# A hybrid decoder layer: the last unit's last eight gathered rows are fetched in two parts

## The reference

```python
# per token and head (8 heads): 16 expert ids and their softmax gates
ue = jnp.take(u_tab, idb, axis=0)
h = jnp.einsum('thkd,td->thk', ue, xb)
act = gb * jax.nn.gelu(h, approximate=False)
ve = jnp.take(v_tab, idb, axis=0)
ffn = jnp.einsum('thk,thkd->td', act, ve)
...
x = layer_norm(DEEPNORM_ALPHA * x + ffn, ln2_g, ln2_b)
gate = jax.nn.sigmoid(x @ ple_wgate + ple_bgate)
x = layer_norm(DEEPNORM_ALPHA * x + gate * (p @ ple_wproj), ln3_g, ln3_b)
```

## Time and profile before

| | |
|---|---|
| three runs, median (lowest to highest) | 1473.62 us (1471.78 to 1478.03) |
| the profiled execution, its own time | 1475.97 us |
| its span, first to last instruction | 1473.9 us |
| busy: PE / DVE / ACT / POOL | 77% / 72% / 64% / 40% of the span |
| DMA queue of the gathers | 536.90 MB, 87.1% of 16 engines' span |
| mean granted TensorE clock | 0.884 |

### The profile page before, as it was taken

One profiled execution on the slowest core, in us unless ns is written; L12 is line 12 of the kernel. 1 busy time (PEld: TensorE's weight loads), 2 busy tenths in 40 slices (PEclk: granted clock), 3 DMA queues, 4 the chain that ended last, 5 costly groups with the idle time before them and its releaser, 6 DMA issues.

```text
span 1473.9 us, 18837 instructions
## 1 busy us (share of the span) xinstructions
PE 1141.0 (77%) x6795; PEld 894.0 (61%) x6795; DVE 1065.0 (72%) x2592; ACT 949.8 (64%) x1613; POOL 584.5 (40%) x528
## 2 busy tenths in 40 slices
PE   8998999988768877787667876786677766677666
PEld 3556777767666667665645555665555655655545
DVE  1378776668778786778756776877886886687765
ACT  2236677678887888766636677667556666666652
POOL 1043344334443444434423444454344444443440
PEclk9999999999899988999767988999888887799888
DMA  9589999999999999999999999999999999999990
GB/s 370 229 320 398 425 417 378 427 427 426 426 427 425 426 424 421 426 427 427 421 429 426 414 423 426 417 418 427 426 421 426 426 425 422 426 418 413 396 426 33
DMA packets 88390, 593.45 MB, mean 403 GB/s; under 512 B 9533, under 2 KB 14309, under 8 KB 19050
## 3 DMA queue, kind: packets, MB, share of 16 engines
q0 software_dynamic: 73728, 536.90, 87.1%
q1 hardware_dynamic: 14570, 55.36, 9.3%
HBM read 590.13 MB, written 2.10 MB: 402 GB/s over the span
## 4 chain that ended last, share of the span: by engine, by line
DMA 42%; PE 29%; ACT 11%; DVE 10%; POOL 4%; issue 4%; SPq 0%; POOLq 0%; DVEq 0%; ACTq 0%
DMA arena<-in_uv,ids 41%; PE ps L1007 10%; DVE arena L1524 6%; PE ps L727 5%; ACT arena L1214 5%; POOL arena L547 4%; PE ps L562 3%; PE ps L909 2%; ACT actv L1209 2%; PE ps L836 2%; PE ps L573 2%; ACT L1206 1%; ACT L1259 1%; ACT gel L1206 1%; PE ps L640 1%
## 5 line engine op out<-in xcount | busy, mean ns | idle before, releaser
L547 POOL DMA_INDIRECT arena<-in_uv,ids x512 | 579.4, 1132 | 811.4 <-PE ps L1007 681.6
L1007 PE MATMUL ps<-ident,arena 128*128 128x128 f32 x4096 | 617.1, 310 | 307.4 <-ACT arena L1214 301.9
L1524 DVE CUSTOM_DVE_ANT_0 arena<-arena 128x1024 f32<-128x1024 f32 x512 | 622.8, 1224 | 287.3 <-DMA arena<-in_uv,ids 279.4
L1007 PEld LDWEIGHTS ps<-ident,arena 128*128 128x128 f32 x4096 | 539.1, 160 | 405.1 <-ACT arena L1214 337.0
L1214 ACT ACTIVATE arena<-arena,actv 128x1024 f32<-128x1024 f32 x511 | 555.8, 1135 | 0.0
L1206 ACT ACTIVATE gel<-hid 128x2 f32<-128x2 f32 (+1 forms) x256 | 51.9, 203 | 387.3 <-DVE hid L1524 381.1
L1209 ACT ACTIVATE actv<-gel,gates 128x1 f32<-128x1 f32 x511 | 122.8, 287 | 8.4
L727 PE MATMUL ps<-arena 128*128 128x128 f32 x992 | 127.3, 291 | 0.0
L727 PEld LDWEIGHTS ps<-arena 128*128 128x128 f32 x992 | 125.3, 209 | 0.0
L1206 ACT ACT_TABLE_LOAD x51 | 65.4, 1283 | 6.8 <-DVE gates L1466 5.9
L836 PE MATMUL ps<-arena 128*128 128x384 f32 x192 | 67.1, 493 | 0.0
(11 more groups left out here) (207 smaller groups left out, 930.5 us busy)
## 6 DMA issues: line engine op xcount, KB each, us to landing
arena<-in_wq SPq DMA_DIRECT2D x20, 1024.0 KB
arena<-in_uv,ids POOLq DMA_INDIRECT x512
arena<-in_w_out SPq DMA_DIRECT2D x2, 2048.0 KB, 16.2
arena<-in_w_gate SPq DMA_DIRECT2D x1, 4096.0 KB
arena<-in_w_out SPq DMA_DIRECT2D x3, 1024.0 KB, 13.4
arena<-in_w_k SPq DMA_DIRECT2D x4, 512.0 KB, 7.0
arena<-in_w_q SPq DMA_DIRECT2D x2, 1024.0 KB, 10.6
arena<-in_w_gv SPq DMA_DIRECT2D x1, 2048.0 KB, 11.9
```

The costliest lines, as they stand in the source:

```text
L547: nc.gpsimd.indirect_dma_start(out=rows[:, c % RING, :], out_offset=None, in_=a["uv"][:, :], in_offset=bass.IndirectOffsetOnAxis(ap=ids[:, ...
L1007: i = mm(ps[:, run_bank(r) + k // 4, (k % 4) * P:(k % 4 + 1) * P], rows[:, c % RING, D + k * P:D + (k + 1) * P], ident[:, :], is_transpose ...
L1524: v.tensor_tensor_reduce(out=r, in0=r, in1=x1[t], scale=1.0, scalar=0.0, op0=ALU.mult, op1=ALU.add, accum_out=hid[:, i, c:c + 1]).then_inc ...
```

## The change

In the last unit the fetches c = 8 to 15 are cut. The main part brings columns 0 to 1535 (all of u and the first half of v, `PART` = 1536, 6 KB a row). Eight further indirect DMAs, issued behind all others, bring the late parts: columns 1536 to 2047, 2 KB a row. ScalarE scales and PE sums only the first half of v for these eight. The second halves are scaled and added up by VectorE in token order (`add_late`: one `tensor_scalar`, then seven `scalar_tensor_tensor` of 128x512, all into `late_sum`); PE then transposes the sum (4 blocks) into bank 5, and VectorE adds it to `acc`. The second half of what PE had summed up to fetch 7 is added to `acc` earlier, beside the last unit (`add_half(1, ...)` at g == 6). The order of PE's tail changes too: the first half of `acc` is transposed back and the first two gate quarters opened before the late sum is there; the second half is transposed back between quarters 2 and 3.

```diff
+LATE = TOPK - RING
+PART = D + HALF
+        late_sum = rows[:, LATE % RING, PART:2 * D]
...
+                    n = PART if u == NU - 1 and c >= LATE else 2 * D
                     nc.gpsimd.indirect_dma_start(
-                        out=rows[:, c % RING, :], out_offset=None, in_=a["uv"][:, :],
+                        out=rows[:, c % RING, 0:n], out_offset=None, in_=a["uv"][:, :],
...
             for u in range(NU):
                 gather_unit(u)
+            for c in range(LATE, TOPK):
+                nc.gpsimd.indirect_dma_start(
+                    out=rows[:, c % RING, PART:2 * D], out_offset=None, in_=a["uv"][:, :],
+                    in_offset=bass.IndirectOffsetOnAxis(ap=ids[:, (NU - 1) % 4, c:c + 1], axis=0),
+                    element_offset=PART,
+                ).then_inc(late_in[c % RING], 16)
...
+                halved = u == NU - 1 and c >= LATE
-                for k in range(KD):
-                    if very_last and k % 4 == 0:
-                        pe.wait_ge(last_scaled, k // 4 + 1)
+                for k in range(KD // 2 if halved else KD):
+                    if very_last and k == 0:
+                        pe.wait_ge(last_scaled, 1)
...
             pe.wait_ge(ple_used, 2 * last)
             pe.wait_ge(score_used, NU)
+            pe.wait_ge(run_added, NR + 1)
+            transposes(4, acc[last], 0).then_inc(y_tr, 1)
             for c, (c0, c1, bank) in enumerate(quarters):
-                if c == 0:
-                    pe.wait_ge(run_added, NR)
+                if c == 2:
+                    pe.wait_ge(late_added, TOPK - LATE)
+                    transposes(5, late_sum, 0).then_inc(last_summed, 1)
+                if c == 3:
+                    pe.wait_ge(run_added, NR + 2)
+                    transposes(5, acc[last], 1).then_inc(y_tr, 1)
                 gate_product(last, c0, c1, 0, KD // 2, bank)
-                if c == 0:
-                    y_transposes(last)
...
-                    r = rows[:, c % RING, D:2 * D]
+                    r = rows[:, c % RING, D:PART if u == NU - 1 and c >= LATE else 2 * D]
...
                     fn(gel[:, i, c:c + 1], hid[:, i, c:c + 1], ACT.Gelu).then_inc(gel_ready, 1)
+                    act.wait_ge(gel_ready, NU * NG + 1)
+                    fn(actv[:, i, c:c + 1], gel[:, i, c:c + 1], ACT.Copy, scale=gates[:, i, c:c + 1])\
+                        .then_inc(actv_ready, 1)
...
+            def add_half(j, bank):
+                half = acc[NT - 1][:, j * HALF:(j + 1) * HALF]
+                v.tensor_tensor(half, ps[:, bank, :], half, ALU.add).then_inc(run_added, 1)
+
+            def add_late(c):
+                r = rows[:, c % RING, PART:2 * D]
+                weight = actv[:, (NU - 1) % 4, c:c + 1]
+                dve.wait_ge(late_in[c % RING], 16)
+                dve.wait_ge(actv_ready, (NU - 1) * TOPK + c + 1)
+                if c == LATE:
+                    v.tensor_scalar(r, r, weight, None, ALU.mult).then_inc(late_added, 1)
                 else:
+                    dve.wait_ge(late_added, c - LATE)
+                    v.scalar_tensor_tensor(out=late_sum, in0=r, scalar=weight, in1=late_sum, op0=ALU.mult, op1=ALU.add)\
+                        .then_inc(late_added, 1)
...
+                    if u == NU - 1 and g == 6:
+                        dve.wait_ge(slot_free, (NU - 1) * TOPK + LATE)
+                        add_half(1, run_bank(NR - 1) + 1)
...
+            add_late(LATE)
             dve.wait_ge(gel_ready, NU * NG + 1)
-            for j in range(2):
-                r = rows[:, c % RING, D + j * HALF:D + (j + 1) * HALF]
-                v.tensor_scalar(r, r, gel[:, i, c:c + 1], gates[:, i, c:c + 1], ALU.mult, ALU.mult)\
-                    .then_inc(last_scaled, 1)
-            add_run(NR - 1)
-            y_stats(last)
+            r = rows[:, c % RING, D:PART]
+            v.tensor_scalar(r, r, gel[:, i, c:c + 1], gates[:, i, c:c + 1], ALU.mult, ALU.mult).then_inc(last_scaled, 1)
+            add_late(LATE + 1)
+            add_late(LATE + 2)
+            dve.wait_ge(last_summed, 1)
+            add_half(0, run_bank(NR - 1))
+            add_late(LATE + 3)
+            add_late(LATE + 4)
+            dve.wait_ge(y_tr, 2 * last + 1)
+            half_stats(ps[:, 4, :], 0)
+            for c in range(LATE + 5, TOPK):
+                add_late(c)
+            dve.wait_ge(last_summed, 2)
+            dve.wait_ge(run_added, NR)
+            add_half(1, 5)
+            dve.wait_ge(y_tr, 2 * last + 2)
+            half_stats(ps[:, 5, :], 1)
             y_var()
             y_centre(last)
             y_rescale(last)
```

More of the change, by code:

```diff
@@ L390, in build @@
         scaled = sem("scaled")
+        late_in = [sem(f"late_in{i}") for i in range(RING)]
+        late_added = sem("late_added")
         last_scaled = sem("last_scaled")
@@ L898, in y_transposes @@
                     pe.wait_ge(ple_used, 2 * i)
-                pe.wait_ge(run_added, NR - RUN_TILE[::-1].index(t) + (1 if i == NT - 1 else 0))
+                pe.wait_ge(run_added, NR - RUN_TILE[::-1].index(t))
                 for j in range(2):
@@ L1001, in combine @@
                 very_last = u * TOPK + c + 1 == NU * TOPK
+                halved = u == NU - 1 and c >= LATE
                 if not very_last:
                     pe.wait_ge(scaled, u * TOPK + c + 1)
-                for k in range(KD):
-                    if very_last and k % 4 == 0:
-                        pe.wait_ge(last_scaled, k // 4 + 1)
+                for k in range(KD // 2 if halved else KD):
+                    if very_last and k == 0:
+                        pe.wait_ge(last_scaled, 1)
                     i = mm(ps[:, run_bank(r) + k // 4, (k % 4) * P:(k % 4 + 1) * P],
                            rows[:, c % RING, D + k * P:D + (k + 1) * P], ident[:, :], is_transpose=True,
[L1009 to L1012, removed]
+                           start=(first and k % 4 == 0), stop=last or (u == NU - 1 and c == LATE - 1 and k >= 4),
+                           skip_group_check=True)
+                if very_last:
+                    i.then_inc(last_summed, 1)
+                else:
                     i.then_inc(slot_free, 1)
@@ L1567, in add_run @@
                 t = RUN_TILE[r]
-                if r < NR - 1:
-                    dve.wait_ge(slot_free, (RUN_END[r] + 1) * TOPK)
+                dve.wait_ge(slot_free, (RUN_END[r] + 1) * TOPK)
                 if RUN_TILE.index(t) == r:
@@ L1572, in add_run @@
                                            op0=ALU.mult, op1=ALU.add).then_inc(run_added, 1)
-                elif r < NR - 1:
+                else:
                     v.tensor_tensor(acc[t], pair(run_bank(r)), acc[t], ALU.add).then_inc(run_added, 1)
-                else:
-                    for j in range(2):
-                        half = acc[t][:, j * HALF:(j + 1) * HALF]
-                        dve.wait_ge(last_summed, j + 1)
-                        v.tensor_tensor(half, ps[:, run_bank(r) + j, :], half, ALU.add).then_inc(run_added, 1)
+            def add_half(j, bank):
[8 more added lines that the diff above has]
+                    v.tensor_scalar(r, r, weight, None, ALU.mult).then_inc(late_added, 1)
+                else:
+                    dve.wait_ge(late_added, c - LATE)
+                    v.scalar_tensor_tensor(out=late_sum, in0=r, scalar=weight, in1=late_sum, op0=ALU.mult, op1=ALU.add)\
+                        .then_inc(late_added, 1)
             def y_stats(i):
```

## The result

The changed kernel is a little slower. Eight runs of each gave medians of 1480.21 us (1476.62 to 1483.95) and, for the kernel before, 1475.45 us (1471.78 to 1480.18); the ratio is 1.0030 with a 95% interval of 1.0016 to 1.0044. So the change costs some 4 us of 1476, within half a percent and still clear of the spread. The profiled execution took 1476.62 us.

What follows compares the result with a forecast made beforehand. The middle was taken as bound by DMA bytes, leaving the tail behind the last landing. Statistics +0.1, clock +0.4 and +1.0 gave +1.5 us: median 1473.62 + 1.5 = 1475.1 us, range 1471.4 to 1479.0.

Steps and rivals of the forecast that it cites:

- its own signs of being wrong: Late issue over 2.2 us, dot 15 landing after 1438, or clock low for more than 6 us behind 1440.
- dot 15: Dot product of the last main part in the last unit: forecast at 1435.7, the part landing 4.91 us earlier.
- The POOL model: Late issues that start inside a dot or late addition end 0.80 us behind it; the last ends about 1442.
- quarter 2 lies in the path: In PE's tail, quarter 2 of the gate products runs between the late sum's transposes and those of half 1; 1.78 us.
- PE's chain from the last addition to the statistics: In the tail: late sum there at 44.9, transposes, quarter 2, transposes of half 1, statistics at 48.6 (times are 1400 +).
- From an issue's end to its landing: Late fetches: 0.7 us until data comes, 0.6 of data, 0.6 from the last byte, together 1.9 us.
- the sum had +0.1 and +0.4 for the clock: End of the second half's statistics: +0.1 us against 1448.47, and +0.4 for a low TensorE clock at quarter 0.
- The second term that was mis-sized: Low TensorE clock in the tail: +0.4 us at quarter 0, +1 at the two-row products and start of the last 32.
- Rival B: Clock stays low longer over quarters 0 to 2, two-row products and half the last 32: 1478 to 1480; chance 0.15.
- Rival A: Gain realised: issues miss the dots, late part lands by 42 (1400 +), clock falls where it fell; -0.5 us, 1473.1; chance 0.25.
- Rival C: Main parts come no faster, fetch 15 lands at 1440.6, late parts 4.9 us later; +4.5, 1478; chance 0.06.
- Rival D: Offset fetches of a quarter row are dear on POOL, from 2.5 us an issue; 1482 or more; chance 0.04.

Runs made afterwards that it cites:

- experiment 3: The changed kernel with PE transposing the second half of acc back before quarter 2; the same run as order; ratio 1.0016 to the kernel before.
- again2: The changed kernel timed and profiled a third time, no edit; ratio 1.0023 to the kernel before.
- no_late: The changed kernel without the eight late fetches and the wait for them, output incomplete; ratio 1.0025 to the kernel before.
- busy: The changed kernel with four more blocks transposed, unread, for each of fetches 8 to 14; ratio 1.0018 to the kernel before.
- same_before: The kernel before, unedited, compared with itself; ratio 0.9999.
- order: The changed kernel with PE transposing the second half of acc back before quarters 2 and 3, not between them; ratio 1.0016 to the kernel before.
- late12_order: The changed kernel with only fetches 12 to 15 cut and the second half of acc transposed back before quarters 2 and 3; ratio 1.0015 to the kernel before.
- busy_order: The changed kernel with the extra transposes of busy and the PE order of order together; ratio 1.0015 to the kernel before.
- late_1kb: The changed kernel with late fetches of 256 columns (1 KB a row), not 512, output incomplete; ratio 1.0021 to the kernel before.

## Why the prediction was wrong

**Two things put the measured time outside the range.** The range ended at 1479.0, the measured median is 1480.21. The baseline of three runs was 1473.62; with eight it is 1475.45, 1.8 us more. And the effect was given as +1.5 us, within 0 and +3, and is +3.8 over the three timings (+4.8 in the first). Both were needed: the measured +4.8 on the low baseline gives 1478.4, and +1.5 on the higher one 1477.0, and both lie inside. The class with the chance of 0.93 came true: it is within half a percent. The expected direction, slightly slower, was right too.

**Of its own signs of being wrong** one came: the clock was low for 6.8 us behind 1440 (1453.5 to 1460.3). No late issue cost over 2.2 us and dot 15 did not land late.

**What held.** Dot 15 at +15.4 against 15.3 forecast. The POOL model: the first five issues locked to the dots' ends, some 1.84 apart, the last of the eight ending at +21.7, +21.9 forecast. The early main parts are given back; quarter 2 lies in the path (0.72 us, as read in experiment 3). PE's chain from the last addition to the statistics, forecast at 3.7 us (44.9 to 48.6), took 3.61. VectorE's and PE's order of events came as written.

**The step that failed first** is the one that reads "From an issue's end to its landing: ... 1.9 us". It added a start-up from the kernel's first gather, 0.6 us of data at the full rate, and 0.6 behind the last byte. In the first profile the seventh part's addition starts 3.98 us behind its issue's end (1438.33 to 1442.31); in again2 the seventh and the eighth take 2.97 and 2.69. Over the seven profiles with eight parts of 2 KB the seventh takes 2.6 to 4.1, and no run tells why it varies. So the seventh part lands at +24.4 in the first profile, 2.1 us behind its forecast of +22.3, and keeps two additions behind it, 1.64 us, of which the forecast had only one. In again2 it was there by +23.4 and the eighth at +24.4. The last addition ends at +26.1, +25.9 and +25.1 where the forecast had +24.5, and the statistics follow it by the same 3.61 us each time. Data of 2 KB rows did not move at 427 GB/s when the queue ran dry; 130 to 270 were seen. Over three profiles of each kernel the statistics end 1.4 us later (27.9 and 29.3 on average), where the sum had +0.1 and +0.4 for the clock. That the landing was mis-sized and bound is shown; that it is what the change costs is not, since no_late without any landing was as slow. The number from the Trainium skill, 2.6 us from start to landing (an estimate from DMA: Bandwidth & Descriptors, "Anatomy of one DMA"), lies further off than the 2.8 from rows; the shortest measured with 2 KB, 3.6, decides.

**The second term that was mis-sized** is the clock. Its mechanism was right at the two-row products, and not at quarters 0 and 1. For the first place I wrote that it costs "half of what it overlaps, about 0.8 us", and took +0.4. In all three profiles of the changed kernel the low stretch, 6.8 us long, was over before quarter 0, which ran at full clock; that term was nothing there. Only three variants had the clock low over these quarters, for 1.1 to 1.3 us, and it set the statistics in one of them (no_late). For the second I wrote "I take +1"; it is 2.0 on average over three profiles of each kernel, from 0.5 to 3.4 against the 10.8 of before. The Trainium skill (TensorE: Matmul & The Clock Gate, Part 1) says that the low clock is the default and activity releases it; by that rule a thinner stretch can stay low for as long as it is thin. The trace of busy agrees, with no low stretch when the work was made up. But the same thin work gave 6.8 us in four profiles and 13.7 in three, and full work gave 6.8 once (same_before), so the rule alone does not give the length. Rival B, the clock, was the nearest of the rivals, in its part behind the mean's transpose; its quarters at half clock did not come.

**The sum, redone.** At the statistics +1.4 where +0.5 was forecast, -0.2 up to the mean's transpose where 0 was, +2.0 behind it where +1.0 was: 3.3 us by three profiles of each kernel, against +1.5. The timings say 3.8; half a microsecond has no place in the tail.

**Rival A** fell: five late issues were caught by dot products, the last part landed behind +24, and even without late landings the statistics came at +28.9. **Rival C** fell: main parts land 1.84 us apart. **Rival D** fell: a late issue costs 0.95 to 1.56 us, no more than others.

**What stays open.** The four variants whose tails are 52.3 to 53.4 (order, late12_order, busy_order) or 53.8 (late_1kb) were timed at 1.0015 to 1.0021, 2 to 3 us, where their tails against the mean of before, 52.7, give -0.4 to +1.1. One tail of each can be off by 1.7 us by the clock, and the intervals reach down to 1.0003; that this explains it was not shown. The later starts of dot 7 would explain it too. No cause in the body was found, and only the semaphores' numbers were tried as one. Nor was a kernel run without both the late landings and the low clock, so how much of the 1.4 us at the statistics can be won back is open.

## What to carry to other kernels

Cutting the last transfers so that what is needed first comes first gains only what the smaller pieces do not cost again: each has its own issue and its own latency, and the last one stands alone at the end of the queue, where no other data hides it. Price a last small fetch by the time from issue to landing, not by its bytes. And work taken off PE just ahead of the tail can be paid for in the tail, at half clock; an idle gap of 2.8 us ahead of the last products cost 2 us here on average. Where two chains end close to each other, taking one away wins little: look at both before you call one the cause. Last, a single profile of so short a tail misleads; compare several.

## What was not expected of the hardware

With little queued ahead, the shortest gathers of 128 rows of 2 KB landed 3.6 to 3.8 us after their issue began and the slowest of the last two some 5.0; the shortest of 1 KB took 3.2. The engines showed some 0.6 of their share and 130 to 270 GB/s in the windows shown. A GpSimd issue that begins inside a VectorE instruction with two SBUF inputs mostly ends 0.8 us behind it: in the trace of the changed kernel 217 of the 242 gather issues that begin inside a dot product end 0.79 to 0.85 us behind its end. It was not always so: the last late issue (1438.63) began 0.09 us inside an addition of that kind (1438.54 to 1439.35), took 0.95 us and ended 0.22 behind it. With dot products 1.84 us apart, the first five late issues came 1.83 to 1.87 us apart. Four extra transposes of 128x128 for each of seven fetches kept the clock at 1.00 from 1432 to 1456 (busy), where without them it was at 0.50 for 6.8 or 13.7 us.
